# RWKV stream: the low part of each weight tile made by GpSimd in four operations of 256 columns in place of one of 1024

## The chip, the cores and the metric

The kernel runs on one core of a Trainium2 chip. The metric is the device time of one execution in microseconds (us), median of several runs. Before the change it is 3502.49 us over three runs (3502.34 to 3505.63).

## The reference, cut to what matters

The program is one layer with two mixers side by side (gated linear attention, "GLA", and RWKV-7), an output product, a short convolution mixer and a mixture of 16 experts. The change touches only the first stage, the RWKV stream. What that stage has to compute, cut from the reference:

```python
h = _rmsnorm(x, norm_w)                       # x: 2048 tokens x 1024
u = (h @ w_in).astype(f32)                    # float32 product, 1024 deep
gla_u, rwkv_u = u[..., :GLA_IN], u[..., GLA_IN:]
...
mixed = shifted_cols + (prev - shifted_cols) * rwkv_mu
r, rk, rv, wl, al = _split(mixed, RWKV_SHIFT_SPLITS)
w = -jax.nn.softplus(-(rwkv_w0 + jnp.tanh(wl) @ rwkv_w_up)) - 0.5
decay = jnp.exp(-jnp.exp(w))
a = jax.nn.sigmoid(rwkv_a0 + al @ rwkv_a_up)
kk = rk * rwkv_k_k                            # then normalised per head
rk = rk * (1.0 + (a - 1.0) * rwkv_k_a)
y = _rwkv7_scan(r_h, decay, k_h, v_h, kk, a)  # recurrence over the tokens, 8 heads of 64
...                                           # group norm, bonus, gate silu(rg)
```

## The kernel before, in words

**Tiles.** The stage works on 16 tiles, numbered i: four groups of 512 tokens times four pairs of heads (HP = 4 pairs). Each tile needs four products of the normalised input with 128 columns of the weights: k, r, v and g. The first tile of each group of tokens needs a fifth one before them, "lr". That makes 68 products, numbered n in the order in which they are computed (`order`).

**Why there is a low part.** A product in full float32 precision is made of three passes of 128x512 matmuls in the faster reduced format: the weights and the input are each split into a high part and a low part, and high x high, high x low and low x high are summed in one PSUM bank. A product has 8 depth blocks times 3 passes, 24 matmuls. The weight tile is 128 partitions x 1024 columns (8 blocks of 128). Its way is: SyncE loads it (`wraw`, "plain_weights" in the profile), ScalarE copies it to the reduced format (`w_hi`, L613), GpSimd subtracts that from the plain tile (`split_lo`, L1144 to L1149, writes `w_lo`), and TensorE waits for semaphore `w_lo` before the first matmul of product n (in `product`, which issues L264, L265 and L266). The low part of product 0 alone is made by VectorE (L1081). There are three buffers of each kind, taken in turn.

**Order of the work.** Every engine's program is written out by hand, in order. A tile is two half tiles; a half tile ("slot" g in the code) is cut into five parts. Each engine does in each part what belongs to the recurrence of an earlier half tile and, between, what belongs to the products of the current tile. For tiles that are not the first of a group, TensorE computes k in parts 1 and 2 and r in parts 3 and 4 of the first half, v in parts 0 and 1 and g in parts 2 and 3 of the second half.

**GpSimd's queue.** GpSimd makes the low part of product n + 2 when product n is finished. When it is k that is finished (part 3 of the first half), the low part is that of v. In the program it stands behind `corner` (L1169 to L1188) and three calls of `level_of` (L1160 and L1161), small operations on 128x128 that prepare the triangular inverse of the next half tile. Behind it stand two more calls of `level_of`, at the start of the next slot. The low parts of g, of the next k and of the next r are made in parts 0, 2 and 4 of the second half. `before_step` (L1154) is one operation of 512 columns per tile.

**VectorE's queue.** In part 4 of the first half VectorE runs `weigh_keys`: L886 (two SBUF inputs), L887 (one SBUF input, scalars), L888 (two SBUF inputs). In the third and fourth tile of each of the first three groups of tokens, `keep_lo` (L848, 1024 columns, two SBUF inputs) follows directly; in the last two tiles `ahead_lo` (L855, the same shape) follows. Then comes `keep_level` (L1036, L1043: one input in SBUF and one in PSUM), which waits for TensorE. `forms_of_k` (L896 to L898, two SBUF inputs) stands in part 1 of the second half, `finish` (L959) in part 0 of the first. L914 is the small operation for which TensorE waits before the second part of product g (`n2_part`).

Of the kernel before, what the change touches and what calls it, by code (L numbers as in the profile page):

```python
# [14 lines left out]
F32 = mybir.dt.float32  # L15
U32 = mybir.dt.uint32
ALU = mybir.AluOpType
# [81 lines left out]
def wait_for(engine, semaphore, value):  # L99

    if not isinstance(value, int) or value > 0:
        engine.wait_ge(semaphore, value)
# [3 lines left out]
def rwkv(nc, k, cols_buf, x, norm_w_col, c_col, w_in, w_up, a_up, cols, mu_lora_col, mT):  # L106
# [7 lines left out]
    with Phase("rw") as ctx:  # L114
# [10 lines left out]
        wraw, w_lo, w_hi = [[whole[:, i * D:(i + 1) * D].rearrange("p (kb n) -> p kb n", n=P) for i in range(3)] for whole in (cols_buf.w, cols_buf.w_lo, cols_buf.w_hi)]  # L125
# [64 lines left out]
        def finished(i, half, part):  # L190

            if i >= NT:
                return ()
            if i % HP == 0:
                return ({1: ("lr",), 2: ("k",)}, {0: ("r",), 2: ("v",), 4: ("g",)})[half].get(part, ())
            return ({3: ("k",)}, {0: ("r",), 2: ("v",), 4: ("g",)})[half].get(part, ())
# [29 lines left out]
        with nc.Block() as block:  # L226
# [914 lines left out]
            @block.gpsimd  # L1141
            def _(pool):
                lm = mk("levels").rearrange("p (l t) -> p l t", t=C)

                def split_lo(n):
                    if n >= len(order):
                        return
                    pool.wait_ge(s["w_hi"], n + 1)
                    nc.gpsimd.tensor_tensor(w_lo[n % 3], wraw[n % 3], w_hi[n % 3].bitcast(F32), ALU.subtract).then_inc(s["w_lo"], 1)  # L1149

                def before_step(i):
                    pool.wait_ge(s["cs"], i + 1)
                    wait_for(pool, s["gate"], i)
                    nc.gpsimd.tensor_tensor(pcs[:], cs[:], sw[:], ALU.subtract).then_inc(s["pcs"], 1)  # L1154

                def level_of(g, l):
                    if g >= 1:
                        pool.wait_ge(s["e"], (g - 1) * LEVELS + l + 1)
                    m = lm[:, l + 1, :].unsqueeze(1).to_broadcast([P, 2, C])
                    nc.gpsimd.tensor_tensor(nt[:, l, 0:2, :], scm[g % 3][:, 0:2, 0, :], m, ALU.mult)  # L1160
                    nc.gpsimd.tensor_tensor(nt[:, l, 2:4, :], across[:], m, ALU.mult).then_inc(s["nt"], 1)  # L1161

                def corner(f):
                    i, u = f // 2, f % 2
                    pool.wait_ge(s["sc_kept"], f + 1)
                    pool.wait_ge(s["n2"], i + 1)
                    nil = scm[f % 3][:, :, 0, :]
                    by_head = nil.rearrange("p (h j) t -> p h j t", h=2)
                    nc.gpsimd.tensor_tensor(by_head, by_head, n2[:, i % 3, 2 * u:2 * u + 2, :].rearrange("p j h -> p h j").unsqueeze(3).to_broadcast([P, 2, 2, C]),  # L1169
                                            ALU.mult).then_inc(s["nil"], 1)  # L1170
                    pool.wait_ge(s["nil"], f + 1)
                    first = lm[:, 0, :].unsqueeze(1).to_broadcast([P, 2, C])
                    both_halves = mk("halves").unsqueeze(1).to_broadcast([P, 2, C])
                    for c in range(2):
                        ins = nc.gpsimd.tensor_copy(across[heads2[1 - c], :, :], scm[f % 3][heads2[c], 2:4, 0, :])
                    ins.then_inc(s["nil_across"], 1)
                    pool.wait_ge(s["nil_across"], f + 1)
                    if f >= 1:
                        pool.wait_ge(s["corner"], f)
                    nc.gpsimd.tensor_tensor(nt0[:, 0:2, :], nil[:, 0:2, :], first, ALU.mult).then_inc(s["nt_raw"], 1)  # L1180
                    nc.gpsimd.tensor_tensor(nt0[:, 2:4, :], across[:], first, ALU.mult).then_inc(s["nt0"], 1)
                    if f >= 2:
                        pool.wait_ge(s["wu"], f - 1)
                    nc.gpsimd.tensor_tensor(inv[f % 2][:, 2:4, 1, :], nil[:, 2:4, :], first, ALU.mult).then_inc(s["t_raw"], 1)
                    pool.wait_ge(s["nt_raw"], f + 1)
                    nc.gpsimd.tensor_tensor(inv[f % 2][:, 0:2, 1, :], nt0[:, 0:2, :], both_halves, ALU.add)
                    pool.wait_ge(s["t_raw"], f + 1)
                    nc.gpsimd.tensor_tensor(inv[f % 2][:, 2:4, 1, :], inv[f % 2][:, 2:4, 1, :], both_halves, ALU.add).then_inc(s["t_turned"], 1)  # L1188

                pool.wait_ge(s["first"], 16 * FIRST)  # L1190
                pool.wait_ge(s["w_lo"], 1)
                split_lo(1)
                for g in slots:
                    i, half = tile_of(g)
                    f = g + 1
                    levels, front = 0 <= g < NG, 0 <= f < NG
                    if levels:
                        level_of(g, 3)
                        level_of(g, 4)
                    for part in range(5):  # L1200
                        if i < NT and (half, part) == ((0, 4) if i % HP == 0 else (0, 2)):
                            before_step(i)
                        if front and part == 3:
                            corner(f)
                            for l in range(3):
                                level_of(f, l)
                        for name in finished(i, half, part):
                            split_lo(windex[(i, name)] + 2)
# [1996 lines left out]
```

## Time and profile before

| | us |
|---|---|
| median of three runs | 3502.49 |
| the profiled execution's own time | 3505.04 |
| its span, first to last instruction | 3503.2 |
| TensorE busy | 3295.7 (94%) |
| VectorE busy | 2185.1 (62%) |
| ScalarE busy | 1462.5 (42%) |
| GpSimd busy | 560.5 (16%) |
| of it the 67 low parts, L1149 | 164.2 |

The RWKV stream takes about the first 900 us of the span. The engines are written PE (TensorE), PEld (its weight loads), DVE (VectorE), ACT (ScalarE), POOL (GpSimd) and SP (SyncE). An entry's duration runs from its start to its end on its engine; time in which it is held up after its start is part of it. Idle time of an engine stands in brackets behind the instruction that ended it, with what released it. GpSimd's entries overlap their successors by some hundredths of a microsecond.

### The profile page before, as it was taken

The numbers are of one execution on the slowest core, as the hardware profiler recorded it, in microseconds if no ns is written. First come the engines' busy times: TensorE is split into PE (matmuls) and PEld (weight loads), VectorE is DVE, ScalarE is ACT, GpSimd is POOL, SyncE is SP. The second block draws the span as 40 slices with busy tenths as digits, with TensorE's granted clock in tenths as the row PEclk, the third lists the DMA queues.
The fourth block names the chain that finished last, engine by engine and source line by source line (L and its number), as shares of the span: only waits on it lengthen the run. The fifth ranks groups of instructions, "written<-read, shape, count | busy, mean of one in ns | idle before, by whom it ended". The sixth has DMA issues, their size and how long they took to land. (4 is left out here: it accounts for less than half of the span.)

```text
span 3503.2 us, 75238 instructions
## 1 busy us (share of the span) xinstructions
PE 3295.7 (94%) x31246; PEld 2824.0 (81%) x31246; DVE 2185.1 (62%) x3701; ACT 1462.5 (42%) x2121; POOL 560.5 (16%) x792
## 2 busy tenths in 40 slices
PE   7999999999699998989989989949999999999997
PEld 5778888788577786867768868849999999999997
DVE  4666766667454655677787766676565656565563
ACT  5445444444255665332232223434444444444442
POOL 3455554555100000000000000000100110011000
PEclk9999999999899999989999999959999999999999
DMA  4221222311233434322121245436666666666662
GB/s 145 56 83 51 66 74 63 83 45 51 66 127 109 145 114 157 132 79 72 61 72 66 79 154 166 151 120 220 208 205 214 201 215 198 214 203 213 205 216 72
DMA packets 361838, 452.90 MB, mean 129 GB/s; under 512 B 15188, under 2 KB 300148, under 8 KB 361588
## 3 DMA queue, kind: packets, MB, share of 16 engines
q1 hardware_dynamic: 350200, 407.40, 35.8%
q0 software_dynamic: 9216, 33.56, 4.1%
q10 hardware_dynamic: 2176, 8.39, 0.6%
q8 instruction: 188, 3.08, 0.4%
q14 instruction: 58, 0.48, 0.0%
HBM read 382.17 MB, written 67.13 MB: 128 GB/s over the span
## 5 line engine op out<-in xcount | busy, mean ns | idle before, releaser
L2852 PE MATMUL bank<-ex_x_hi,ex_w_lo 128*128 128x256 f32 x2048 | 581.4, 284 | 2.0 <-DVE ex_x_lo L3034 2.0
L2854 PE MATMUL bank<-ex_x_hi,ex_w_hi 128*128 128x256 f32 x2048 | 580.1, 283 | 0.0
L2853 PE MATMUL bank<-ex_x_lo,ex_w_hi 128*128 128x256 f32 x2048 | 580.1, 283 | 0.0
L2848 DVE TENSOR_TENSOR ex_w_lo<-ex_w_loaded,ex_w_hi 128x2048 fp32r<-128x2048 f32 x192 | 434.0, 2289 | 226.8 <-ACT ex_w_hi L2844 222.3
L2844 ACT ACTIVATE ex_w_hi<-ex_w_loaded 128x2048 fp32r<-128x2048 f32 x192 | 359.4, 1904 | 173.2 <-PE bank L2854 169.3
L2852 PEld LDWEIGHTS bank<-ex_x_hi,ex_w_lo 128*128 128x128 f32 x2048 | 393.6, 192 | 2.8 <-issue 2.2
L2853 PEld LDWEIGHTS bank<-ex_x_lo,ex_w_hi 128*128 128x128 f32 x2048 | 393.7, 192 | 0.6
L2854 PEld LDWEIGHTS bank<-ex_x_hi,ex_w_hi 128*128 128x128 f32 x2048 | 393.7, 192 | 0.0
L2326 PE MATMUL bank<-sc_tokens_hi,sc_w_lo 128*128 128x512 f32 x672 | 268.0, 399 | 27.2 <-DVE hidden_hT_split L2439 10.5
L2908 POOL CAST ex_idx<-moe_idx_all 128x2 uint32 (+1 forms) x16 | 3.0, 188 | 1750.8 <-POOLq L79 1439.3
L2328 PE MATMUL bank<-sc_tokens_hi,sc_w_hi 128*128 128x512 f32 x672 | 265.8, 396 | 0.0
L264 PE MATMUL bank<-columns_columns_hi,weights_weights_lo 128*128 128x512 f32 x544 | 226.7, 417 | 9.5 <-DVE columns_columns_lo L848 4.4
L3008 ACT ACTIVATE ex_hid_hi<-ex_hidden 128x256 fp32r<-128x256 f32 x128 | 53.4, 417 | 414.1 <-DVE ex_hidden L3057 414.1
L759 ACT ACTIVATE rw_E<-bank 128x256 f32<-128x256 f32 x160 | 61.2, 382 | 378.6 <-PE bank L371 378.6
L266 PE MATMUL bank<-columns_columns_hi,weights_weights_hi 128*128 128x512 f32 x544 | 213.9, 393 | 0.0
L265 PE MATMUL bank<-columns_columns_lo,weights_weights_hi 128*128 128x512 f32 x544 | 213.6, 393 | 0.0
L2852 PE MATMUL bank<-ex_w_hi,ex_hid_lo 128*128 128x512 f32 x512 | 200.8, 392 | 0.0
L2854 PE MATMUL bank<-ex_w_hi,ex_hid_hi 128*128 128x512 f32 x512 | 199.4, 390 | 0.0
L2853 PE MATMUL bank<-ex_w_lo,ex_hid_hi 128*128 128x512 f32 x512 | 199.2, 389 | 0.0
L1149 POOL TENSOR_TENSOR weights_weights_lo<-plain_weights,weights_weights_hi 128x1024 fp32r<-128x1024 f32 x67 | 164.2, 2450 | 206.8 <-ACT weights_weights_hi L613 206.6
L2326 PEld LDWEIGHTS bank<-sc_tokens_hi,sc_w_lo 128*128 128x128 f32 x672 | 128.8, 192 | 59.8 <-issue 13.5
L3057 DVE TENSOR_TENSOR ex_hidden<-ex_silu,bank 128x256 f32<-128x256 f32 x128 | 53.5, 418 | 157.0 <-PE bank L2854 157.0
(485 smaller groups left out, 8314.9 us busy)
## 6 DMA issues: line engine op xcount, KB each, us to landing
ex_w_loaded<-in_wg SPq DMA_DIRECT2D x64, 1024.0 KB, 5.4
ex_w_loaded<-in_wu SPq DMA_DIRECT2D x64, 1024.0 KB, 6.2
ex_w_loaded<-in_wd SPq DMA_DIRECT2D x64, 1024.0 KB, 5.1
plain_weights<-in_w_in SPq DMA_DIRECT2D x70, 512.0 KB, 4.6
gl_ada_tile<-in_ada_w SPq DMA_DIRECT2D x48, 512.0 KB, 4.2
hidden_first_w<-in_sc_w_in SPq DMA_DIRECT2D x24, 1024.0 KB, 5.1
plain_columns<-hT_dram SPq DMA_DIRECT2D x14, 1024.0 KB, 7.4
plain_columns<-in_x SPq DMA_DIRECT2D x16, 512.0 KB, 5.5
```

Source lines behind the costliest of these rows:

```text
L264: nc.tensor.matmul(psum, lo[:, kb, :], h_hi[:, :, at], start=(kb == 0), stop=False)
L265: nc.tensor.matmul(psum, hi[:, kb, :], h_lo[:, :, at], start=False, stop=False)
L266: mm = nc.tensor.matmul(psum, hi[:, kb, :], h_hi[:, :, at], start=False, stop=(kb == KD - 1))
L759: nc.scalar.activation(eb[:], k.psum[:].rearrange("p (i x) -> p i x", x=512)[:, 4:6, 256:384].rearrange("p i (j t) -> p i j t", t=C), ACT. ...
L1149: nc.gpsimd.tensor_tensor(w_lo[n % 3], wraw[n % 3], w_hi[n % 3].bitcast(F32), ALU.subtract).then_inc(s["w_lo"], 1)
L2326: nc.tensor.matmul(psum, w_lo[:, at, kb, :], hi[:, kb, :], start=(kb == 0 and not more), stop=False, skip_group_check=more)
L2328: mm = nc.tensor.matmul(psum, w_hi[:, at, kb, :], hi[:, kb, :], start=False, stop=(kb == H - 1), skip_group_check=more)
L2844: nc.scalar.activation(w_hi[c % SPLIT][:], raw[:, c % LOADED, :], ACT.Copy).then_inc(s["hi"], 1)
L2848: nc.vector.tensor_tensor(w_lo[c % SPLIT][:], raw[:, c % LOADED, :], w_hi[c % SPLIT][:].bitcast(F32), ALU.subtract).then_inc(s["lo"], 1)
L2852: nc.tensor.matmul(psum, ll, rh, start=first, stop=False)
L2853: nc.tensor.matmul(psum, lh, rl, start=False, stop=False)
L2854: return nc.tensor.matmul(psum, lh, rh, start=False, stop=last)
```

## The change

In `split_lo`, the one subtraction over 8 blocks of 128 columns is replaced by four subtractions over 2 blocks each. The wait for `w_hi` stands ahead of the first one, and the increment of `w_lo` is on the last one.

```diff
                     pool.wait_ge(s["w_hi"], n + 1)
-                    nc.gpsimd.tensor_tensor(w_lo[n % 3], wraw[n % 3], w_hi[n % 3].bitcast(F32), ALU.subtract).then_inc(s["w_lo"], 1)
+                    for piece in range(4):
+                        kbs = slice(2 * piece, 2 * piece + 2)
+                        ins = nc.gpsimd.tensor_tensor(w_lo[n % 3][:, kbs], wraw[n % 3][:, kbs], w_hi[n % 3][:, kbs].bitcast(F32), ALU.subtract)
+                    ins.then_inc(s["w_lo"], 1)
```

No instruction changes its place among the others. Every line of the kernel behind the change has a number that is 3 higher (L1160 becomes L1163), and the subtraction of L1149 is at L1151. GpSimd issues 268 subtractions where it issued 67.

On GpSimd, around the low part of a v product (L1149), which stands between the third and the fourth pair of level operations (`rw_nt`), before:

```order
L1160 TENSOR_TENSOR rw_nt<-rw_scores,mixers_masks 128x128
L1161 TENSOR_TENSOR rw_nt<-rw_nil_across,mixers_masks 128x128
L1149 TENSOR_TENSOR weights_weights_lo<-plain_weights,weights_weights_hi 128x1024 [waits rw_w_hi]
L1160 TENSOR_TENSOR rw_nt<-rw_scores,mixers_masks 128x128
L1161 TENSOR_TENSOR rw_nt<-rw_nil_across,mixers_masks 128x128
```

The same place in the changed kernel:

```order
L1163 TENSOR_TENSOR rw_nt<-rw_scores,mixers_masks 128x128
L1164 TENSOR_TENSOR rw_nt<-rw_nil_across,mixers_masks 128x128
L1151 TENSOR_TENSOR weights_weights_lo<-plain_weights,weights_weights_hi 128x256 [waits rw_w_hi]
L1151 TENSOR_TENSOR weights_weights_lo<-plain_weights,weights_weights_hi 128x256 x3
L1163 TENSOR_TENSOR rw_nt<-rw_scores,mixers_masks 128x128
L1164 TENSOR_TENSOR rw_nt<-rw_nil_across,mixers_masks 128x128
```

One entry has become four, of which the first alone waits; what stands ahead and behind is the same.

## Rows read from the trace of the kernel before

**Rows 1.** 50 to 850 us: busy us (count) of PE, PEld, DVE, ACT, POOL; clock, DMA.

```profile
50.00:850.00 800.00, 783.62 (x14278) 638.40 (x14280) 519.53 (x1101) 374.40 (x696) 427.49 (x601) 1.00 0.23 64
```

**Rows 2.** Durations of L1149: ns min/median/max, first and last start in us.

```profile
L1149 POOL TENSOR_TENSOR weights_weights_lo<-plain_weights,weights_weights_hi x67: 2350/2379/2818, 16.8 to 843.8; 128x1024 fp32r<-128x1024 f32 x67
```

**Rows 3.** GpSimd's groups by shape: count, busy us, mean ns, idle before.

```profile
L1154 POOL TENSOR_TENSOR rw_tanh_g_or_cs_before<-rw_cs,rw_sw 128x512 f32<-128x512 f32 x16 | 20.6, 1284 | 91.2 <-DVE rw_cs L880 91.2
L1169 POOL TENSOR_TENSOR rw_scores<-rw_scores,inus_half_inverse_square 128x256 f32<-128x256 f32 x32 | 19.7, 615 | 141.1 <-DVE rw_scores L1022 141.1
...
L1181 POOL TENSOR_TENSOR rw_nt<-rw_nil_across,mixers_masks 128x128 f32<-128x128 f32 x32 | 13.3, 414 | 0.0
```

**Rows 4.** Durations of L887 on VectorE, columns as in rows 2.

```profile
L887 DVE TENSOR_SCALAR rw_a<-rw_a,rw_derived x16: 545/2470/2476, 54.4 to 838.5; 128x512 f32<-128x512 f32 x16
```

**Rows 5.** Timeline of all engines, 403 to 409 us: start, duration, instruction.

```profile
404.43 2.81 POOL L1149 TENSOR_TENSOR weights_weights_lo<-plain_weights,weights_weights_hi 128x1024 fp32r<-128x1024 f32 x1
...
405.05 2.47 DVE L887 TENSOR_SCALAR rw_a<-rw_a,rw_derived 128x512 f32<-128x512 f32 x1
...
407.20 0.59 POOL L1160 TENSOR_TENSOR rw_nt<-rw_scores,mixers_masks 128x128 f32<-128x128 f32 x1
...
407.56 0.78 DVE L888 TENSOR_TENSOR rw_a<-rw_a,rw_kx 128x512 f32<-128x512 f32 x1
...
407.75 0.86 POOL L1161 TENSOR_TENSOR rw_nt<-rw_nil_across,mixers_masks 128x128 f32<-128x128 f32 x1
...
408.38 1.32 DVE L848 TENSOR_TENSOR columns_columns_lo<-plain_columns,columns_columns_hi 128x1024 fp32r<-128x1024 f32 x1
...
408.71 0.48 PE L264 MATMUL bank<-columns_columns_hi,weights_weights_lo 128*128 128x512 f32 x1
```

**Rows 6.** Timeline of VectorE, 404 to 413.5 us.

```profile
413.03 0.69 DVE L1049 TENSOR_TENSOR rw_WU<-bank,inus_half_inverse_square 128x512 f32<-128x512 f32 x1 [1.89 <-PE bank L403]
```

**Rows 7.** Timeline of all engines, 786 to 790.5 us.

```profile
786.36 2.81 POOL L1149 TENSOR_TENSOR weights_weights_lo<-plain_weights,weights_weights_hi 128x1024 fp32r<-128x1024 f32 x1
...
789.79 0.50 PE L264 MATMUL bank<-columns_columns_hi,weights_weights_lo 128*128 128x512 f32 x1
...
790.31 1.32 DVE L855 TENSOR_TENSOR columns_columns_lo<-plain_columns,columns_columns_hi 128x1024 fp32r<-128x1024 f32 x1
```

**Rows 8.** Timeline of all engines, 297.5 to 302 us.

```profile
297.61 2.81 POOL L1149 TENSOR_TENSOR weights_weights_lo<-plain_weights,weights_weights_hi 128x1024 fp32r<-128x1024 f32 x1
...
301.04 0.50 PE L264 MATMUL bank<-columns_columns_hi,weights_weights_lo 128*128 128x512 f32 x1
...
301.44 0.41 DVE L1036 TENSOR_TENSOR rw_inverse<-rw_inverse,bank 128x256 f32<-128x256 f32 x1
```

**Rows 9.** Timeline of all engines, 83 to 86 us.

```profile
83.22 2.36 POOL L1149 TENSOR_TENSOR weights_weights_lo<-plain_weights,weights_weights_hi 128x1024 fp32r<-128x1024 f32 x1
...
85.72 0.47 PE L264 MATMUL bank<-columns_columns_hi,weights_weights_lo 128*128 128x512 f32 x1 [1.42 <-POOL weights_weights_lo L1149]
```

**Rows 10.** Timeline of all engines, 54 to 63 us.

```profile
54.63 2.53 POOL L1149 TENSOR_TENSOR weights_weights_lo<-plain_weights,weights_weights_hi 128x1024 fp32r<-128x1024 f32 x1 [5.84 <-ACT weights_weights_hi L613]
...
54.95 2.76 DVE L888 TENSOR_TENSOR rw_a<-rw_a,rw_kx 128x512 f32<-128x512 f32 x1
...
57.75 0.69 DVE L896 TENSOR_TENSOR rw_PR<-rw_PR,rw_kk 128x512 f32<-128x512 f32 x1
...
57.78 0.48 PE L264 MATMUL bank<-columns_columns_hi,weights_weights_lo 128*128 128x512 f32 x1
...
59.03 2.38 POOL L1149 TENSOR_TENSOR weights_weights_lo<-plain_weights,weights_weights_hi 128x1024 fp32r<-128x1024 f32 x1 [1.87 <-ACT weights_weights_hi L613]
...
59.08 2.88 DVE L898 TENSOR_TENSOR rw_KT<-rw_KT,rw_a 128x512 f32<-128x512 f32 x1
...
62.22 0.50 PE L264 MATMUL bank<-columns_columns_hi,weights_weights_lo 128*128 128x512 f32 x1 [1.47 <-DVE rw_square_sum L914]
```

**Rows 11.** Waits of TensorE, 50 to 850 us: total us, times, longest us.

```profile
PE bank L416 <- DVE plain_columns L839: 3.3, 6, 0.6
```

## The prediction

> **What bounds the kernel now.** I read the busy time by stretch first. From 50 to 850 us, nearly the whole RWKV stream, TensorE is busy 783.6 of 800 us at the full granted clock (1.00, the level of 2.4 GHz), VectorE 519.5 and GpSimd 427.5 [rows 1]. So TensorE bounds the stage, and a change on GpSimd counts only through what TensorE waits for. The waits of TensorE come next: the greatest on another engine that recurs with VectorE's work is L416, 3.3 us in six waits [rows 11]. Two single waits, 1.42 and 1.47 us, stand in the timeline [rows 9, 10]. Then the group of L1149: 67 operations, median 2379 ns, longest 2818 [rows 2]. The reader is to see in the timeline round one of the long ones [rows 5] that two engines hold each other up. VectorE's L887 takes 545 ns where nothing runs beside it and 2470 ns in most places [rows 4]; it begins at 405.05, but ends at 407.52, 0.28 us after L1149 has ended (407.24). The other way round, L1161 on GpSimd takes 0.86 us and not 0.41, and ends 0.27 us after L888. Last, the distance from the end of a low part to the first matmul of its product. It is short for the v products, whose low part stands behind the level operations in GpSimd's queue: 1.47 us [rows 5], 0.62 [rows 7] and 0.62 [rows 8].
>
> The Trainium skill (SBUF — State Buffer, section "SBUF: two separate sides") says that VectorE operations with two SBUF inputs, or in a two-port mode, and GpSimd operations share one pair of ports as an exclusive lock, held for the whole instruction, which blocks the other. The trace agrees for L887 and L888.
>
> **What a piece costs.** The trace has no subtraction of 256 columns with two full inputs. From 512 to 1024 columns the duration grows by 2379 - 1284 = 1095 ns [rows 2, 3], 2.14 ns per column; 256 columns would be 736 ns. From 128 (414 ns) to 512 columns it grows by 2.27 ns per column, which gives 704 ns. The one row with 128x256, L1169, has 615 ns, but one of its inputs is a broadcast. A queued GpSimd operation starts 0.04 us before the former one ends (407.20 against 407.24). So four pieces take 4 x 0.704 - 3 x 0.04 = 2.70 us, by the other rows 2.34 to 2.82, against 2.38. I take 0.35 us more per tile, nearest to the rows with two full inputs, so 0.68 us per piece; the bounds are -0.04 and +0.44. On GpSimd that is 67 x 0.35 = 23 us, beside 373 us in which it idles [rows 1], and where a low part has room ahead of its product it costs nothing. A page makes the piece's price slightly different: the Trainium skill (Perfetto Trace Analysis, section "GPSIMD Engine Instruction") says to time this engine by the spacing of starts and not by reported durations. By durations alone the four pieces would be 2.82 to 2.94 us, some 0.1 us more at each place below.
>
> **What it moves: VectorE gets in between the pieces.** Between L1160 and L1161, both queued, L888 got its turn; L1161 got its own after it [rows 5]. I take it that the engines alternate in the same way at each boundary between pieces. Here is the place at 404 us, from the ends in rows 5. L1149 truly ran from 407.24 - 2.38 = 404.86. Piece 1 ends at 405.54. L887 ends 0.28 later, 405.82. Piece 2 ends 0.27 + 0.29 = 0.56 later (0.27 is what L1160 and L1161 need behind a VectorE operation, 0.29 the longer piece), 406.38. L888 ends 0.55 after a GpSimd operation, 406.93. Piece 3: 407.49. L848 ends 1.09 after (409.70 against 408.61), 408.58. Piece 4: 409.14. The low part is complete 1.90 us later than at 407.24. VectorE is 1.1 us earlier (408.58 against 409.70).
>
> **What TensorE loses.** The shortest distance from the low part's end to the matmul, where TensorE truly waits, is 85.72 - 85.58 = 0.14 us [rows 9]. So the margin at 404 us is 1.47 - 0.14 = 1.33, and the wait would be 0.57 us. There are five v products of this kind, in tiles 3, 6, 7, 10 and 11: 2.85 us. In tiles 14 and 15 L855 stands in L848's place, as long and as ready, and the margin is 0.62 - 0.14 = 0.48 [rows 7]: 1.42 us each, 2.84 together. In tiles 5, 9 and 13 nothing with two SBUF inputs follows L888; L1036 does, which reads one input from PSUM [rows 8]. There piece 4 follows piece 3 at 0.66, the delay is 0.91 and the wait 0.43: 1.29 together. In tile 1 TensorE waits already and no such VectorE operation comes near: +0.35 [rows 9]. Tile 2, whose L848 falls beside the low part as a whole, has a delay about equal to its margin; I take it at zero. Behind each late low part stand in GpSimd's queue two calls of `level_of`, whose results TensorE reads half a slot later; they hold nobody up.
>
> **What TensorE gains.** In the first tile it waits 1.47 us at 62.22 for L914, which is late because L898 (2.88 us) sits behind the L1149 of 59.03 [rows 10]. With pieces L898 is done after the first one, near 60.3, and that wait goes. But before that the low part of g (54.63) lets L888 in, and then L896 and its like, three at 0.55 us, so it ends some 1.5 us later, at 58.7; the matmul of 57.78 moves by 1.5 - 0.62 + 0.14 = 1.0 us. Net -0.5 us. In the steady state VectorE's lead of 1.1 us reaches nobody: before L1049 it idles 1.89 us for TensorE [rows 6], and L839, for which L416 waits, comes behind L1049.
>
> **Sum.** 2.85 + 2.84 + 1.29 + 0.35 - 0.5 = 6.8 us. The profiled execution of before took 3505.0 us with a span of 3503.2; a profile of after should show about 3511.9 and 3510.0. The median of before, 3502.5, is 2.5 lower, and a wait of TensorE is as long there: 3509.3 us.
>
> **The rivals.** (a) The pieces run on as one: queued GpSimd operations keep the ports, L887 stays at 2.47. Then only 0.35 us per tile is left, under every margin but tile 1's: 3502.5 + 0.35 = 3503, or 3501 if the first tile gains. Against it stands L888 between L1160 and L1161. (b) VectorE gets in, but not at every boundary: GpSimd runs two pieces in a turn at times, L848 comes behind piece 4, and every place has only the 0.91 us of tiles 5, 9 and 13. For it speaks that the rows show single operations taking turns, never four of one wait. Tiles 3 to 11 of the first kind then wait for nothing, tiles 14 and 15 0.43 each: 1.29 + 0.86 + 0.35 - 0.5 = 2.0, 3504.5 us. (c) Faster: VectorE's lead does reach TensorE. The mechanism is L887 released 1.7 us earlier, L839 earlier by as much, and the six waits of L416 gone; price 3.3 us, with 1.47 of the first tile: 3502.5 - 4.8 = 3497.7. It decides only if the lead outlives the idle 1.89 us before L1049, which the profile speaks against, and if the low parts are not late as well. (d) Each change of turn costs more: VectorE's whole durations (0.55 + 0.78 + 1.32) and 0.44 per tile, so 3.1 us at seven places and 1.8 at three: waits of 1.77 x 5 + 2.6 x 2 + 1.3 x 3 = 18 us, 3520.
>
> **How the numbers follow.** Within 0.2% is within 7.0 us, about what a measurement of this kernel can tell from no change. Chances: the forecast 0.50 (3506 to 3512), (a) 0.17, (b) 0.17, (c) 0.05, (d) 0.11. The forecast lies at the edge, so half of its chance goes to "no change": 0.25 + 0.17 + 0.17, and 0.01 from (c), 0.60; slower has the other half and (d), 0.36; faster 0.04, the rest of (c), whose 4.8 us reach 7 only with some more. The range that leaves out most of (c) and the upper half of (d) is 3501 to 3515.
>
> **What would show it.** L887 in a profile of after: near 0.8 us in ten places and not 2.47; if it stays, (a) holds. The four pieces at 404 us: together 4.3 us from first start to last end, with L888 and L848 between them; under 3.4 means (b). L264 with idle time released by GpSimd: some ten waits, 0.4 to 1.4 us, in place of one. The wait at 62.22 gone. L416's six waits should stay near 3.3 us; if they shrink, (c) is at work. The prediction is wrong if the time moves by under 3 us, or if stages behind 900 us move.

## The result, and the profile after

The changed kernel takes 3513.52 us, median of 8 runs (3502.64 to 3518.66), the kernel before 3503.36 us in the same comparison (3501.46 to 3506.31). The ratio is 1.0026 with a 95% interval of 1.0015 to 1.0036: slower by 5 to 13 us. The forecast was 6.8 us slower, 3509.3 us. The profiled execution of after took 3518.66 us, 5 us above its median.

The busy times of TensorE, VectorE, ScalarE and GpSimd in the stage, with a stretch 20 us longer than in [rows 1]; the last columns are TensorE's granted clock and the DMA:

```profile
50.00:870.00 820.00, 796.74 (x14488) 648.51 (x14488) 511.01 (x1113) 377.12 (x702) 457.84 (x793) 1.00 0.22 62
```

VectorE is busy for less time than before over a longer stretch, GpSimd for more. The durations (ns min/median/max) that answer to [rows 2, 4], from the views of the two lines:

```profile
L1151 POOL TENSOR_TENSOR weights_weights_lo<-plain_weights,weights_weights_hi x268: 714/732/1717, 17.1 to 856.8; 128x256 fp32r<-128x256 f32 x134
...
L887 DVE TENSOR_SCALAR rw_a<-rw_a,rw_derived x16: 545/844/846, 56.0 to 849.1; 128x512 f32<-128x512 f32 x16
```

A piece takes 732 ns, and L887 is held up for 0.3 us where it was held up for 1.9. Now the place that answers to [rows 5], from the timeline of all engines. The four pieces are merged into one row, since they follow each other:

```profile
410.19 4.86 POOL L1151 TENSOR_TENSOR weights_weights_lo<-plain_weights,weights_weights_hi 128x256 fp32r<-128x256 f32 x4
...
410.81 0.85 DVE L887 TENSOR_SCALAR rw_a<-rw_a,rw_derived 128x512 f32<-128x512 f32 x1
411.69 1.10 DVE L888 TENSOR_TENSOR rw_a<-rw_a,rw_kx 128x512 f32<-128x512 f32 x1
412.82 1.64 DVE L848 TENSOR_TENSOR columns_columns_lo<-plain_columns,columns_columns_hi 128x1024 fp32r<-128x1024 f32 x1
...
415.20 0.47 PE L264 MATMUL bank<-columns_columns_hi,weights_weights_lo 128*128 128x512 f32 x1 [0.47 <-POOL weights_weights_lo L1151]
```

The low part took 2.81 us from start to end and takes 4.86: all three VectorE operations now run inside it. TensorE's first matmul of the product, which followed 1.47 us behind it, now waits for it. The places that answer to [rows 9], [rows 8] and [rows 7], in order of time:

```profile
86.03 2.77 POOL L1151 TENSOR_TENSOR weights_weights_lo<-plain_weights,weights_weights_hi 128x256 fp32r<-128x256 f32 x4
...
88.95 0.47 PE L264 MATMUL bank<-columns_columns_hi,weights_weights_lo 128*128 128x512 f32 x1 [1.79 <-POOL weights_weights_lo L1151]
...
301.84 3.87 POOL L1151 TENSOR_TENSOR weights_weights_lo<-plain_weights,weights_weights_hi 128x256 fp32r<-128x256 f32 x4
...
305.86 0.47 PE L264 MATMUL bank<-columns_columns_hi,weights_weights_lo 128*128 128x512 f32 x1 [0.46 <-POOL weights_weights_lo L1151]
...
795.41 4.86 POOL L1151 TENSOR_TENSOR weights_weights_lo<-plain_weights,weights_weights_hi 128x256 fp32r<-128x256 f32 x4
...
798.04 1.63 DVE L855 TENSOR_TENSOR columns_columns_lo<-plain_columns,columns_columns_hi 128x1024 fp32r<-128x1024 f32 x1
...
800.41 0.47 PE L264 MATMUL bank<-columns_columns_hi,weights_weights_lo 128*128 128x512 f32 x1 [1.48 <-POOL weights_weights_lo L1151]
```

The first pair shows the pieces with no VectorE operation that holds them up: 2.77 us against 2.36. At 301 us only L887 and L888 get in. The first tile, as in [rows 10]; the eight pieces are those of products 4 and 5:

```profile
56.30 7.95 POOL L1151 TENSOR_TENSOR weights_weights_lo<-plain_weights,weights_weights_hi 128x256 fp32r<-128x256 f32 x8 [7.10 <-ACT weights_weights_hi L613]
...
60.04 1.10 DVE L898 TENSOR_TENSOR rw_KT<-rw_KT,rw_a 128x512 f32<-128x512 f32 x1
...
60.74 0.47 PE L264 MATMUL bank<-columns_columns_hi,weights_weights_lo 128*128 128x512 f32 x1 [1.15 <-POOL weights_weights_lo L1151]
...
61.18 0.17 DVE L914 TENSOR_SCALAR rw_square_sum<-bank 128x8 f32<-128x8 f32 x1
```

L898 takes 1.10 us where it took 2.88, and the wait for L914 is gone, but a wait for the low part stands ahead of it. Last, TensorE's waits in the stage (total us, times, longest), which answer to [rows 11], and VectorE's idle time before L1049, as in [rows 6]:

```profile
PE bank L264 <- POOL weights_weights_lo L1151: 9.8, 12, 1.8
...
PE bank L416 <- DVE plain_columns L839: 3.3, 6, 0.6
```

```profile
419.50 0.69 DVE L1049 TENSOR_TENSOR rw_WU<-bank,inus_half_inverse_square 128x512 f32<-128x512 f32 x1 [3.59 <-PE bank L403]
```

L416's six waits have not moved, and VectorE idles 3.59 us where it idled 1.89: its lead has become idle time.

**Where the time went.** I compared the start of every TensorE matmul with the start of the same matmul in the trace before. The lag between the two grows in steps at L264, the first matmul of a product:

```
place (time before)                 lag grows by, us
first tile, 57.8                    +1.29
first tile, 62.2 (L914)             -1.62
v of tile 1, 85.7                   +0.38
v of tile 2, 136.2                  +0.32
v of tiles 3, 6, 7, 10, 11          +0.72 +0.71 +0.72 +0.72 +0.72
v of tiles 5, 9, 13                 +0.53 +0.57 +0.57
v of tiles 14, 15                   +1.55 +1.56
sum                                 +8.74
```

The sum is 8.7 us: 9.08 us at the v products (tile 1 and the eleven from tile 2 on), less 0.33 in the first tile.

The whole lag grows by more than these steps, by 10.4 us from 50 to 870 us. Nearly all of the rest is one stretch of 3.4 us, from 61.1 us on, in which TensorE was granted the low level of its clock (0.50, the level of 1.2 GHz; the rows stand at after_again below) and lost about 1.6 us. The trace before has no such stretch between 50 and 870 us.

### The profile page after: what moved, and what is told of

It reads as the page before. It is cut to its first block and busy times, and to the rows that moved or that the text cites. A ratio compares the mean times of both kernels' runs of the same rounds, so it can differ in the third digit from the quotient of the medians.

```text
span 3516.8 us, 75439 instructions
## 1 busy us (share of the span) xinstructions
PE 3299.0 (94%) x31246; PEld 2826.4 (80%) x31246; DVE 2172.8 (62%) x3701; ACT 1461.9 (42%) x2121; POOL 593.2 (17%) x993
## 5 line engine op out<-in xcount | busy, mean ns | idle before, releaser
L1151 POOL TENSOR_TENSOR weights_weights_lo<-plain_weights,weights_weights_hi 128x256 fp32r<-128x256 f32 x268 | 214.9, 832 | 197.2 <-ACT weights_weights_hi L613 197.1
L264 PE MATMUL bank<-columns_columns_hi,weights_weights_lo 128*128 128x512 f32 x544 | 227.4, 418 | 16.5 <-POOL weights_weights_lo L1151 9.8
```

The costliest lines, as they stand in the source:

```text
L264: nc.tensor.matmul(psum, lo[:, kb, :], h_hi[:, :, at], start=(kb == 0), stop=False)
L1151: ins = nc.gpsimd.tensor_tensor(w_lo[n % 3][:, kbs], wraw[n % 3][:, kbs], w_hi[n % 3][:, kbs].bitcast(F32), ALU.subtract)
```

## The experiments

Theory: VectorE's queued operations get in between the pieces, this makes low parts late, and TensorE pays where the low part had little room. The main rival is a price per added GpSimd operation, wherever it stands.

**v_whole: the low part of v in one operation.**

```diff
-                    for piece in range(4):
-                        kbs = slice(2 * piece, 2 * piece + 2)
+                    count = 1 if order[n][1] == "v" else 4
+                    for piece in range(count):
+                        kbs = slice(piece * KD // count, (piece + 1) * KD // count)
```

> The low parts of the v products are made in one operation as before, all others in four pieces. Theory (VectorE's queued operations get in between the pieces, and only the low parts of v have so little room that TensorE then waits): the waits of TensorE at v, 9.1 us together in the changed kernel's profile, are gone, and the time is 3504.5 us (3503 to 3506). Rival (each added GpSimd operation costs about the same wherever it stands, 10 us over 201 operations): 150 of 201 are still there, 3511 us. Second rival (TensorE's clock is low for longer, without the waits being the cause): no change against 3513.5.

Measured: 3503.47 us, ratio to before 1.0002 (0.9993 to 1.0011). TensorE's waits for low parts fall to two:

```profile
PE bank L264 <- POOL weights_weights_lo L1152: 2.5, 2, 1.4
```

They are the one of the first tile and that of tile 1, which the kernel before has too. The whole loss is gone while three quarters of the added operations are still there. A price per operation wherever it stands is out, and so is a clock that is low without the waits.

**v_only: the low part of v alone in four pieces.** The edit is that of v_whole with `count = 4 if order[n][1] == "v" else 1`.

> Only the low parts of the v products are made in four pieces, all others in one operation. Theory: the waits at v stay whole, and the median is 3512 to 3513 us, with the wait for L914 at 62 us back (1.5 us). Rival (a price per added operation): 48 of 201, 3505.9 us. L264's waits for GpSimd: theory 9 us, rival near the 1.4 us of the kernel before.

Measured: 3511.13 us, ratio 1.0025 (1.0013 to 1.0037).

```profile
PE bank L264 <- POOL weights_weights_lo L1152: 8.8, 11, 1.8
...
PE bank L264 <- DVE rw_square_sum L914: 1.5, 1, 1.5
```

With 48 of 201 added operations the loss is 7.4 us of medians, within the interval of the changed kernel's. In its profile the lag grows by 8.8 us in the stage, and there is no low stretch of the clock in it. Together the two kernels put it on the v products from both sides.

**two: two pieces of 512 columns everywhere.** The same edit with `count = 2`.

> Every low part is made in two pieces of 512 columns. Theory: at a v product only one boundary lies inside the low part, so only L887 gets in: 0.28 us for it, some 0.15 us more for the second operation, 0.4 to 0.5 us late against margins of 0.48 us and more. TensorE waits nowhere but in tile 1, 3503.5 to 3504.5 us. L887 takes about 1.4 us and not 2.47 (before) or 0.84 (four pieces). Rival (a price per added operation, 67 of 201): 3506.8 us.

Measured: 3498.92 us, ratio 0.9990 (0.9981 to 0.9999). At the place of [rows 5], timeline of all engines:

```profile
404.15 3.15 POOL L1152 TENSOR_TENSOR weights_weights_lo<-plain_weights,weights_weights_hi 128x512 fp32r<-128x512 f32 x2
...
404.77 1.39 DVE L887 TENSOR_SCALAR rw_a<-rw_a,rw_derived 128x512 f32<-128x512 f32 x1
```

One boundary, one VectorE operation in it: L887 takes 1.39 us and the low part 0.34 us more than 2.81, less than even the smallest of the margins, 0.48. L264 waits for GpSimd once (1.5 us). The mechanism is as expected; the median is 5 us under what I expected. The trace has only 1.6 us of that, at L914; the rest is within the interval, and I don't explain it.

**eight: eight pieces of 128 columns everywhere.** The same edit with `count = 8`.

> Every low part is made in eight pieces of 128 columns. Theory: the same three VectorE operations get in, no more, and the eight pieces take some 0.2 to 0.3 us more than four: each of the 12 waits at v grows by that, 3516 to 3517 us. Rival (a price per added operation, 469 against 201): 3527 us.

Measured: 3529.10 us, ratio 1.0075 (1.0061 to 1.0089). The time is the rival's number and not mine.

```profile
PE bank L264 <- POOL weights_weights_lo L1152: 17.0, 12, 2.4
...
PE bank L354 <- POOL rw_nt L1185: 2.4, 4, 0.7
```

The waits at v did grow, but by 0.56 us each in the middle places (0.72 to 1.28) and not by 0.2 to 0.3. The mistake is the price of an operation: I took the 414 ns of the masked operations on 128 columns for a subtraction that takes 457:

```profile
L1152 POOL TENSOR_TENSOR weights_weights_lo<-plain_weights,weights_weights_hi x536: 443/457/1437, 17.1 to 867.7; 128x128 fp32r<-128x128 f32 x179
```

A whole low part takes, from its first start to its last end (the median over the products), 2.38, 2.52, 2.81 and 3.40 us in one, two, four and eight pieces: 0.145 us per added operation, on a straight line. Four more than in the changed kernel are 0.58 us, the 0.56 seen. The lag against before grows by 15.8 us at the v products, 0.9 in the first tile and 1.3 at three L354, which now wait for GpSimd behind a long low part. Nearly 6 us more of lag come in four stretches of 3.4 us at the low clock level, one at each of the four waits of over 2 us (below); the changed kernel had one such stretch. So a price per operation is real, but v_whole shows that it is paid only where the low part is on TensorE's path.

**lo_late: L848 and L855 one part later in VectorE's program.** Four pieces everywhere.

```diff
-                    for n in split_in(i, half, part, 4):
-                        keep_lo(n)
-                    for n in ahead_in(i, half, part, 4):
-                        ahead_lo(n)
+                    if half == 1 and part == 1:
+                        for n in split_in(i, 0, 4, 4):
+                            keep_lo(n)
+                        for n in ahead_in(i, 0, 4, 4):
+                            ahead_lo(n)
...
```

> Four pieces everywhere as in the changed kernel, but in VectorE's program the low part of the input (keep_lo, ahead_lo; L848, L855) of part 4 of the first half stands behind L1036 and L1043 of the next slot, one part later. Theory (L848 and L855 hold the ports between pieces 3 and 4): the waits at v in tiles 3, 6, 7, 10, 11 (0.7 us each) and 2 (0.3) go, those in tiles 14 and 15 fall from 1.55 to about 0.6, together 5.7 us: 3508 us. Rival (the price is that of the pieces alone, or L888's): the time stays at 3513.5 and the waits as they are.

Measured: 3509.47 us, ratio 1.0018 (1.0009 to 1.0027). TensorE's waits, and the place at 405 us in the timeline of all engines:

```profile
PE bank L264 <- POOL weights_weights_lo L1157: 5.5, 7, 1.8
```

```profile
405.11 3.88 POOL L1157 TENSOR_TENSOR weights_weights_lo<-plain_weights,weights_weights_hi 128x256 fp32r<-128x256 f32 x4
...
409.40 0.48 PE L264 MATMUL bank<-columns_columns_hi,weights_weights_lo 128*128 128x512 f32 x1
```

The low part takes 3.88 us and not 4.86, and the waits of tiles 3, 6, 7, 10 and 11 are gone (12 waits to 7), with the 0.32 us of lag at tile 2. Those of tiles 14 and 15 fall to the 0.5 us of tiles 5, 9 and 13. L848 in the last boundary is worth 0.98 us of lateness. By the lags this kernel loses 2.7 us to the one before in the stage; its median is 5.0 us higher (3.2 to 9.5 by the interval), and the rest I don't explain.

**narrow888: L888 on 8 columns.** Four pieces everywhere.

```diff
-                    go.put(nc.vector.tensor_tensor(a[:], a[:], kx[:], ALU.mult))
+                    go.put(nc.vector.tensor_tensor(a[:, 0:8], a[:, 0:8], kx[:, 0:8], ALU.mult))
```

> Four pieces everywhere, and L888, which multiplies all 512 columns, multiplies only the first 8: the scaling of the other 504 columns of k is left out. Theory: L888 holds the ports for some 0.05 us and not 0.55, the low part of v is complete 0.5 us earlier, and the ten waits at v fall by 0.5 us each (0.7 to 0.2, 0.57 to 0.1, 1.55 to 1.05): 3508.5 us. Rival (only the pieces' own length counts): waits unchanged, 3513.5 us.

Measured: 3507.72 us, ratio to before 1.0007 (0.9998 to 1.0016).

```profile
PE bank L264 <- POOL weights_weights_lo L1151: 4.2, 4, 1.4
```

```profile
404.75 4.42 POOL L1151 TENSOR_TENSOR weights_weights_lo<-plain_weights,weights_weights_hi 128x256 fp32r<-128x256 f32 x4
```

At the place of [rows 5] (second row, timeline of all engines) the low part takes 4.42 us and not 4.86. The waits at tiles 14 and 15 fall from 1.48 and 1.50 to 1.04 us, and those of tiles 3, 5, 6, 7, 9, 10, 11 and 13 fall under what the view counts (0.15 us). So L888 too holds up the pieces: what was taken from it is worth 0.44 us (0.5 expected). The pieces are as many as before and as long by themselves, so the rival is out.

**after_again: the changed kernel a second time.**

> The changed kernel once more, for a second profile. Its profiled execution was 5 us above its median, with stretches at the low clock level (half the full one) near 61 and 996 us that the kernel before did not have. Theory (the ten waits at v are fixed, the low stretches differ from execution to execution): the waits of L264 for GpSimd are 9 to 10 us again, and the low stretches stand elsewhere, so that the span is 3508 to 3515 us. Rival (the low stretch at 61 us follows from the wait at 60.7): it is there again.

Measured: 3514.22 us, ratio 1.0024 (1.0015 to 1.0033), span 3511.7 us.

```profile
PE bank L264 <- POOL weights_weights_lo L1151: 9.9, 12, 1.8
```

The twelve waits are the same. The granted clock of the stretch 61.2 to 64.4 us (third column from the end) is 0.50 in the first profile and 1.00 in the second, which has a low stretch at 87 us in its place. First profile, then second:

```profile
61.20:64.40 3.20, 3.20 (x10) 2.42 (x9) 3.01 (x6) 0.05 (x1) 3.05 (x4) 0.50 0.24 71
```

```profile
61.20:64.40 3.20, 3.20 (x16) 2.62 (x15) 3.04 (x5) 0.00 (x0) 2.75 (x4) 1.00 0.14 41
87.10:90.30 3.20, 3.20 (x8) 2.52 (x9) 0.18 (x1) 1.08 (x2) 3.20 (x7) 0.50 0.02 5
```

The rival, that the low stretch at 61 us must follow the wait at 60.7, is out as a rule; both stretches do lie right beside a wait of over 1 us. Each costs about 1.6 us, so the lag grows by 10.0 us from 50 to 870 us here and by 10.4 in the first profile.

**n5_only: product 5 alone in four pieces.** The edit of v_whole with `count = 4 if n == 5 else 1`.

> Only the low part of product 5 (the k product of tile 1, made at 59 us) is in four pieces, all 66 others in one operation. Theory (VectorE's L898 gets in after the first piece, and L914, for which TensorE waits 1.47 us at 62.2, is 1.6 us earlier): that wait is gone, 1.5 us faster than before, 3501.9 us, which a timing can hardly tell, but the profile can. Rival: L898 stays behind all four pieces and the wait stays.

Measured: 3499.77 us, ratio 0.9986 (0.9975 to 0.9996). In the timeline of all engines:

```profile
59.17 1.24 DVE L898 TENSOR_TENSOR rw_KT<-rw_KT,rw_a 128x512 f32<-128x512 f32 x1
...
60.44 0.17 DVE L914 TENSOR_SCALAR rw_square_sum<-bank 128x8 f32<-128x8 f32 x1
```

L898 takes 1.24 us and not 2.88, and the wait of 1.47 us is gone; the lag to before falls by 1.63 us there and nowhere else in the stage by as much. The median fell by 4.7 us, the interval reaches from 1.4 to 8.8. The trace supports 1.6 of it.

**early4 and early_n5: the low part of v earlier in GpSimd's queue.**

```diff
-                        if front and part == 3:
-                            corner(f)
-                            for l in range(3):
-                                level_of(f, l)
+                        inside = front and part == 3
+                        if inside:
+                            corner(f)
+                            level_of(f, 0)
                         for name in finished(i, half, part):
                             split_lo(windex[(i, name)] + 2)
+                        if inside:
+                            level_of(f, 1)
+                            level_of(f, 2)
```

> Four pieces everywhere, but in GpSimd's program the low part of v stands behind the first call of level_of for the next half tile and ahead of the second and third, so it begins 1.5 to 1.7 us earlier. Theory (the pieces cost time only where the low part is late in GpSimd's queue): the ten waits at v (0.7, 0.57 and 1.55 us) and the one of tile 1 (1.8) go, the wait of 1.15 at 60 us stays and the wait for L914 is gone: 3513.5 - 11 = 3502.5 us. Rival (VectorE and GpSimd hold each other up as long as before, and TensorE now waits for the second and third level operations instead, L368 for GpSimd): 3508 us or more.

> The low part of product 5 is in four pieces and all others in one operation, and the low part of v stands behind the first call of level_of, as in the other kernel of this pair. Theory: the waits of 1.47 us (L914, at 62 us) and 1.42 us (low part of v, tile 1) are both gone, 3.0 us under the kernel before, 3501.4 us by its 3504.4; no other wait appears. Rival: the one of tile 1 comes back as a wait for the level operations, and the time is that of the kernel with product 5 in pieces alone.

Measured: early4 3500.68 us, ratio 0.9994 (0.9984 to 1.0004); early_n5 3500.28 us, ratio 0.9994 (0.9985 to 1.0003). In early4 TensorE waits twice for a low part, at 60 us and for 0.36 us in tile 1; in early_n5 not at all. early4:

```profile
PE bank L264 <- POOL weights_weights_lo L1151: 1.5, 2, 1.2
```

At the place of [rows 5], timeline of all engines of early4:

```profile
402.48 3.72 POOL L1151 TENSOR_TENSOR weights_weights_lo<-plain_weights,weights_weights_hi 128x256 fp32r<-128x256 f32 x4
...
403.38 1.09 DVE L949 TENSOR_TENSOR rw_Y<-rw_Y,rw_group_stat 128x512 f32<-128x512 f32 x1
404.50 1.11 DVE L886 SCALAR_TENSOR_TENSOR rw_kk_a_or_y_square<-rw_a,rw_kk 128x512 f32<-128x512 f32 x1
405.65 0.83 DVE L887 TENSOR_SCALAR rw_a<-rw_a,rw_derived 128x512 f32<-128x512 f32 x1
```

The edit did two things. The low part begins some 1.7 us earlier, and it meets other VectorE operations: L949 and L886 get in and L887 falls at its end, while L888 and L848 come behind it, so it takes 3.72 us and not 4.86. It ends 2.52 us ahead of its first matmul here and 1.66 us ahead in tiles 5, 9, 13, 14 and 15. The room alone would have been enough: with the old 4.86 us the low parts of tiles 14 and 15 would still end some 0.5 us ahead (an estimate: 1.66 - 1.14), where TensorE needs 0.14. No wait for a level operation has come in its place. Against the changed kernel's 1.0024 to 1.0026 this gives the 10 us back. Both medians lie some 3 us under that of the kernel before in the same comparison (3503.73), but neither can be told from it.

## Why the prediction was right

**Direction, size and place.** 6.8 us were forecast and 10.2 measured (5 to 13 by the interval). The time of 3513.5 us lies in the range of 3501 to 3515, but above the 3506 to 3512 to which the forecast gave its chance of 0.50: the mechanism was right and the size too small. The step that carried it, that the engines take turns at every boundary, is shown: L887 went to 0.844 us in ten places (forecast near 0.8), and v_whole, v_only, lo_late and narrow888 take the loss away, keep it, or reduce it as their waits say.

**Price of a piece: under-sized.** I took 0.117 us per added operation, 0.35 per low part. It is 0.145, so 0.44 by the medians 2.38 and 2.81; that was the upper bound, from the row of 512 columns. The row of 128 columns, to which I leaned, is a masked operation and takes 414 ns where the subtraction takes 457.

**The waits, term by term.** Tiles 3, 6, 7, 10, 11: forecast 2.85, lag 3.59 us. Tiles 14, 15: 2.84 against 3.12. Tiles 5, 9, 13: 1.29 against 1.68. Tile 1: 0.35 against 0.38. Tile 2: zero against 0.32. The first tile: -0.5 against -0.33, and both of its parts as foretold, a new wait for the low part of g and the old one for L914 gone. From tile 3 on each v term is short by 0.10 to 0.15 us per place, of which the piece's price is 0.09. The sum by the lags is 8.7 and not 6.8.

**VectorE's lead.** It reached nobody: L416's waits stayed at 3.3 us and the idle time before L1049 grew from 1.89 to 3.59. Rival (c) is out but for its part in the first tile, which is in the sum, and that alone is what n5_only keeps.

**The rivals (a), (b) and (d).** (a) fell with L887 at 0.844. (b) fell with L848 inside the four pieces. The two lengths given as signs were wrongly worked out: 4.3 us counts from the corrected start at 404.86, but a row starts at 404.43, so the same working gives 4.71 there (measured 4.86), and (b) would have shown 2.81 + 0.91 = 3.72 us and not under 3.4. Tiles 5, 9 and 13, where L1036 follows L888, show just that form, with 3.87. (d) is off by size: the lateness is 2.05 us and not 3.1.

**A term put at nothing: the clock.** The forecast has no term for TensorE's granted clock. In both profiles of the changed kernel one stretch of 3.4 us at the low level stands in the stage, and each adds about 1.6 us to the 8.7 us of the steps. Together that is 10.3 us, beside 10.2 us between the medians. The last sign, that nothing behind 900 us moves, holds: from 880 us to the end the lag changes by +0.9 us in one profile and -3.1 in the other.

**What stays open.** Whether most executions of the changed kernel have one such stretch, as the two profiled ones do, is not shown; v_only, with nearly the same waits, has none in its profile, and by medians it loses 7.4 us and not 10.2, a difference that lies within the intervals. The first profiled execution of after has a span 13.6 us longer than that of before. Of this 10.4 us lie in the stage, 1.7 in the first 50 us and the rest behind the stage. Over the first 1100 us the low level lasted 41 us in the profile before, 55 in that of after and 48 in the second one; outside the stage such stretches differ from execution to execution.

## What to carry to other kernels

Where two engines hold each other up, cutting an operation of the one into pieces lets the other in between; the first one's result is then late by everything that gets in, plus a price per added piece (0.145 us here). So cut where the held-up engine is waited for and the cut result has room, as at product 5, and leave whole what the bounding engine needs next. Before cutting, list for each place the distance from the result's end to its first use: one edit of the order that started the low part some 1.7 us earlier was worth the whole loss.

## What the runs showed of the hardware

The turns are strict at the v products: behind each piece came the one VectorE operation that was queued, and behind it the next piece (L887, L888, L848 in the three boundaries of four pieces, and in the first three of eight). L887 takes its turn like the others, though only one of its inputs is a full tile in SBUF. Operations that read one input from PSUM (L1036, L1043) ran at their usual 0.41 us beside GpSimd's: in the kernel before, the 50 of them that lie wholly inside a low part take 0.41 to 0.42 us.

TensorE was granted the low level, for 3.4 us each time, right behind or beside some of its waits. In eight that happened at all four waits of over 2 us (2.17 us at 60.5, 2.36 at 89.3, 2.06 at 808.3, 2.03 at 863.5):

```profile
61.80:65.00 3.20, 3.20 (x9) 2.53 (x8) 0.36 (x1) 0.00 (x0) 2.75 (x6) 0.50 0.00 0
89.10:92.30 3.20, 3.02 (x7) 2.47 (x8) 0.17 (x1) 0.84 (x1) 3.20 (x10) 0.50 0.02 5
809.30:812.40 3.10, 3.10 (x9) 2.31 (x7) 0.00 (x0) 0.00 (x0) 3.10 (x8) 0.50 0.00 0
864.00:867.00 3.00, 3.00 (x8) 2.32 (x8) 0.00 (x0) 0.00 (x0) 3.00 (x9) 0.50 0.02 5
```

The last two each added 1.6 us to the lag, so that a wait of 2.1 us cost 3.7. Of the 22 waits of 1.1 to 1.9 us that TensorE has in the stage in the other eleven profiles, two had such a stretch beside them: the one of 1.15 us at 60.7 in after and the one of 1.83 us at 87.0 in after_again. Waits of the same length in the same places had none in v_whole, v_only, lo_late and early4.
